# POOL multiplies the gates into nine of sixteen one-hot batches, and the first group of expert blocks takes no fetched rows

## The reference, cut to what matters

```python
q = (xb @ w_query).reshape(tb, PEER_HEADS, 2, PEER_HALF)           # 8 heads, two halves of 128
s = jnp.einsum('thpc,hpnc->thpn', q, sub_keys)                     # 128 keys per half
top_s, top_i = lax.top_k(s, PEER_TOPK)                             # 16 best of each half
cand_s = top_s[:, :, 0, :, None] + top_s[:, :, 1, None, :]         # 16 x 16 sums
best_s, best_pos = lax.top_k(cand_s, PEER_TOPK)                    # 16 best pairs
idx = jnp.take_along_axis(cand_i, best_pos, axis=-1)               # expert = key0 * 128 + key1
g = jax.nn.softmax(best_s, axis=-1)
h = gelu(jnp.einsum('thkd,td->thk', expert_u[idx], xb))
out = jnp.einsum('thk,thkd->td', g * h, expert_v[idx])             # 128 experts per token
```

## Time and profile before

| what | before |
|---|---|
| median of 3 runs | 2973.97 us |
| profiled execution, its own time | 2976.31 us |
| its span, first to last instruction | 2974.5 us |
| PE busy | 2643.6 us (89%) |
| DVE busy | 2434.8 us (82%) |
| ACT busy | 871.1 us (29%) |
| POOL busy | 1254.2 us (42%) |
| mean granted clock of TensorE | 0.939 |

### The profile page before, as it was taken

One profiled execution on the slowest core, in us unless ns is written; L12 is line 12 of the kernel. 1 busy time (PEld: TensorE's weight loads), 2 busy tenths in 40 slices (PEclk: granted clock), 3 DMA queues, 4 the chain that ended last, 5 costly groups with the idle time before them and its releaser, 6 DMA issues.

```text
span 2974.5 us, 47235 instructions
## 1 busy us (share of the span) xinstructions
PE 2643.6 (89%) x17293; PEld 1732.6 (58%) x17459; DVE 2434.8 (82%) x4517; ACT 871.1 (29%) x1463; POOL 1254.2 (42%) x833
## 2 busy tenths in 40 slices
PE   8999888698867674589999999999999999999996
PEld 3566655458867663445555555555555555555553
DVE  3244545574999999589999999999999999999998
ACT  2333333211114444522222222222222222222223
POOL 2110000210000000066666666676667677776772
PEclk9999979799988985689999999999999999999998
DMA  4000010261002223699999999999999999999994
GB/s 153 22 15 15 15 71 15 93 244 48 1 1 114 113 103 160 251 374 351 361 350 353 342 357 344 338 356 347 335 345 337 348 331 350 342 337 338 335 333 177
DMA packets 262960, 685.26 MB, mean 230 GB/s; under 512 B 35624, under 2 KB 118184, under 8 KB 258352
## 3 DMA queue, kind: packets, MB, share of 16 engines
q0 software_dynamic: 110592, 402.70, 36.2%
q1 hardware_dynamic: 152240, 280.98, 26.9%
HBM read 624.89 MB, written 58.72 MB: 230 GB/s over the span
## 4 chain that ended last, share of the span: by engine, by line
PE 20%; issue 13%; DVE 11%; DMA 10%; POOL 2%; SPq 1%; DVEq 0%; ACT 0%; POOLq 0%
PE o_psum L1879 10%; PE h_psum L1861 10%; DMA early<-v_blocks,pick_index 6%; DMA fetched<-v_blocks,pick_index 3%; DVE wide L1731 3%; DVE early L1727 2%; DVE early L1702 2%; DVE v_split L1713 1%; POOL early L1670 1%; DVE wide L1719 1%; DMA fetched<-u_rows,pick_index 1%; DVE act_out L1690 1%; DVE w_split L1694 1%; SPq L2009 1%; POOL fetched L1670 1%
## 5 line engine op out<-in xcount | busy, mean ns | idle before, releaser
L1861 PE MATMUL h_psum<-early 128*128 128x384 bf16 (+1 forms) x6144 | 863.2, 301 | 25.5 <-issue 14.9
L1879 PE MATMUL o_psum<-v_split,w_split 128*128 128x512 bf16 x3713 | 826.9, 380 | 24.6 <-DVE wide L1719 13.4
L1861 PEld LDWEIGHTS h_psum<-early 128*128 128x128 bf16 x6144 | 604.0, 98 | 284.2 <-issue 31.7
L1879 PEld LDWEIGHTS o_psum<-v_split,w_split 128*128 128x128 bf16 x3840 | 375.4, 98 | 456.3 <-DVE wide L1719 18.5
L1670 POOL DMA_INDIRECT early<-v_blocks,pick_index x320 | 488.7, 1527 | 225.4 <-DVE wide L1731 137.4
L1670 POOL DMA_INDIRECT early<-u_rows,pick_index x320 | 448.3, 1401 | 320.1 <-DVE dots L1727 201.5
L1731 DVE SCALAR_TENSOR_TENSOR wide<-early,dots,wide 128x1024 f32<-128x1024 f32 x320 | 402.2, 1282 | 37.3 <-DMA early<-v_blocks,pick_index 33.6
L1727 DVE CUSTOM_DVE_ANT_0 early<-early,wide 128x1024 f32<-128x1024 f32 x320 | 382.1, 1217 | 36.5 <-DMA early<-u_rows,pick_index 31.5
L1617 ACT ACTIVATE w_split<-act_out 128x640 bf16<-128x640 f32 x128 | 94.3, 737 | 633.5 <-DVE act_out L1690 582.2
L1604 ACT ACTIVATE act_out<-h_psum 128x384 f32<-128x384 f32 (+1 forms) x256 | 97.6, 433 | 597.1 <-PE h_psum L1861 546.9
L1101 PE MATMUL r_t_psum<-rt_x_t,early 128*128 128x128 f32 (+1 forms) x1920 | 236.7, 285 | 0.0
(11 more groups left out here) (201 smaller groups left out, 2976.3 us busy)
## 6 DMA issues: line engine op xcount, KB each, us to landing
early<-u_blocks SPq DMA_DIRECT2D x128, 512.0 KB
early<-v_blocks SPq DMA_DIRECT2D x128, 512.0 KB
gates<-wide SPq DMA_DIRECT2D x20, 2048.0 KB, 6.4
gate<-gates SPq DMA_DIRECT2D x32, 1280.0 KB
early<-w_query SPq DMA_DIRECT2D x8, 1024.0 KB, 5.8
att_w_raw<-w_fox SPq DMA_DIRECT2D x4, 1536.0 KB, 6.8
early<-u_rows,pick_index POOLq DMA_INDIRECT x320
early<-v_blocks,pick_index POOLq DMA_INDIRECT x320
```

The lines of the kernel that those rows point to most:

```text
L1861: mm = pe.matmul(h_psum[k][:, half, 0:width * P], u_split[:, k, part, c], xs[:, first:first + width, xpart, c, :], start=(c == 0 and part ...
L1879: mm = pe.matmul(o_psum[(DENSE * p + t) % 2][:, half * 512:half * 512 + 512], w_split[:, p, q, part, t * P:(t + 1) * P], v_split[:, p, q, ...
```

## The change

**Routing.** In the four steps that also hold picks, POOL takes over the multiplication by the gates: for batches 0, 1, 2 and 15 whole (2048 elements), for batches 4 to 8 its low half (1024 elements), and DVE keeps the high half. PE waits for the new semaphore `hot_by_pool` as well. DVE keeps the is_equal of all batches, and everything of the fifth tile.

**Experts.** No row is taken in the first group. From unit 5 on (`FIRST_UNIT`) the 384 U rows are spread evenly to unit 82 (`MIDDLE_UNIT`), and the 384 V rows from there to unit 160. The six first fetches are issued as early as before. DVE's program for the 32 groups is now written out, with no loop.

```diff
+        POOL_BOTH, POOL_LOW = (0, 1, 2, 15), (4, 5, 6, 7, 8)
...
                 def gate_batch(d, m):
                     n = SLOTS * d + m
-                    pe.wait_ge(hot_made, n + 1)
+                    if m in POOL_SLOTS and shared(d):
+                        pe.wait_ge(hot_by_pool, len(POOL_SLOTS) * d + POOL_SLOTS.index(m) + 1)
...
+                def gate_batch(d, m):
+
+                    n, slot, first = SLOTS * d + m, m % HOTS, 0 if m in POOL_BOTH else 1
+                    pool.wait_ge(high_made, n + 1)
+                    pool.tensor_tensor(hot[:, slot, 2 + first:4],
+                                       hot[:, slot, 0].unsqueeze(1).broadcast_to(
+                                           [P, 2 - first, BATCH // 2, N_KEYS, 2]),
+                                       by_pair(gates_t[:, m, first:2].rearrange("p k n -> p (k n)")).rearrange(
+                                           "p (k j) n two -> p k j n two", k=2 - first), ALU.mult
+                                       ).then_inc(hot_by_pool, 1)
...
+                    if m in POOL_BOTH and shared(d):
+                        return
+                    halves = 1 if m in POOL_LOW and shared(d) else 2
                     dve.wait_ge(high_made, n + 1)
...
+    WEIGHED = GROUP * groups // 2 + 2
+    FIRST_UNIT, MIDDLE_UNIT = DENSE, DENSE * (WEIGHED // GROUP) + WEIGHED % GROUP
...
+                def due(unit):
+
+                    if unit <= FIRST_UNIT:
+                        return 0
+                    if unit <= MIDDLE_UNIT:
+                        return TAKES // 2 * (unit - FIRST_UNIT) // (MIDDLE_UNIT - FIRST_UNIT)
+                    return TAKES // 2 + TAKES // 2 * (unit - MIDDLE_UNIT) // (DENSE * groups - MIDDLE_UNIT)
...
-                dve.wait_ge(acc_in, 16 * GATHERED)
-                pair(0, "U")
-                with dve.Fori(1, TURNS) as i:
-                    pair(i, "U")
-                pair(TURNS, "V")
-                with dve.Fori(TURNS + 1, last) as i:
-                    pair(i, "V")
-                pair(last, "V")
+                taken = [0]
+                for g in range(groups):
+                    group_of_blocks(g)
```

More of the change, by code:

```diff
@@ L1263, in step @@
                     for m in range(SLOTS):
[L1264 to L1269, removed]
+                        if not (isinstance(d, int) and d == DENSE):
+                            if m == PRODUCTS_SLOT - 3:
+                                products(t)
+                            if m == PRODUCTS_SLOT - 2:
+                                float_index(t)
+                        if m in POOL_SLOTS and shared(d - 1):
+                            gate_batch(d - 1, m)
                 pool.sem_inc(floated, 1)
@@ L1720, in add, with take @@
                                              ).then_inc(o_added, 1)
[L1722 to L1727, removed]
+                def take(n):
+                    tile, i, k, row = n % GATHERED, n // PICKS, n % PICKS // GATHERED, fetched[n % RING]
+                    dve.wait_ge(fetched_in[n % RING], 16 * (n // RING + 1))
+                    if n < TAKES // 2:
+                        dve.tensor_tensor_reduce(row, row, acc[:, tile], 1.0, 0.0,
@@ L1744, in load_dots, with take_until @@
                     dve.wait_ge(weights_copied, i - TURNS + 1)
[L1746 to L1751, removed]
-                    for q in range(GROUP):
-                        gate_block(GROUP * g + q, g, p, q, n)
-                        split_u_lo(i, GROUP * g + q + 2, GROUP * p + q)
-                        split_v_lo(GROUP * g + q, p, q, GROUP * i + (GROUP * p + q) // 2 + 1)
-                        if p == 0 and q == 0 and kind == "V":
-                            load_dots(i)
+                def take_until(last_take):
+                    for n in range(taken[0], last_take):
+                        if n == 0:
+                            dve.wait_ge(acc_in, 16 * GATHERED)
+                        if n >= TAKES // 2 and n % PICKS == 0:
+                            load_dots(n // PICKS)
+                        take(n)
+                    taken[0] = max(taken[0], last_take)
@@ L1758, in step @@
                         for t in DOWN_TILES[q]:
-                            units += 1
-                            upto = (half * units - half // 2) // DENSE
-                            for r in range(taken, upto):
-                                take(i, kind, half * p + r)
+                            take_until((due(unit) + due(unit + 1)) // 2)
                             if t == DOWN_TILES[q][0]:
-                                split_w_lo(GROUP * g + q, p, q)
-                            if not (first and p == 0):
-                                if t == 0 and first:
+                                split_w_lo(b, p, q)
@@ L1767, in step @@
+                            if g > 0:
+                                if t == 0 and g == 1:
                                     dve.wait_ge(dense_in, 16 * DENSE)
@@ L1769, in step @@
                                     dve.wait_ge(o_added, DENSE * (g - 1))
[L1770 to L1783 removed]
+                                add(g - 1, 1 - p, t, ALPHA if g == 1 else 1.0)
+                            unit += 1
+                            take_until(due(unit))
                 def weigh():
```

63 lines of the change are left out of this document (34 added, 29 removed).

## The result

| what | before | after |
|---|---|---|
| median of 4 runs each, same chip | 2976.97 us | 2947.49 us |
| lowest and highest | 2970.5 to 2981.79 | 2942.5 to 2952.44 |
| profiled execution, own time | 2976.31 us | 2942.5 us |
| its span | 2974.5 us | 2940.7 us |
| mean granted clock | 0.939 | 0.942 |

The ratio is 0.9898 with the interval [0.9874, 0.9922]: 1.0% faster, where I had said 2972 us, in a range of 2952 to 2994. The forecast was wrong.

The account below looks back on a forecast made before the run. DVE was taken to set the routing's pace, transfers the experts' start, and DVE to be no less tight than PE afterwards. Routing -3.7 and experts +2.4 gave -1.3 us on 2976.3, so 2972 us as median, range 2952 to 2994.

Parts of the forecast that it names:

- The rival that POOL's products cost DVE nothing: Routing: DVE and POOL take no turns, so -25 us, 2951 us as median; chance 0.08.
- my own chain of slots 0 to 2: Routing, batches 0 to 2: is_equal 1.2, plus 0.1, plus POOL's product 4.25 gives 5.6 us between is_equals.
- what the sums and the cast take from DVE where they cut in: Routing, batches 3 and 4: POOL's late sums and cast delay DVE by their full length, +1.5 and +0.9 us.
- slot 15: Routing: batch 15's product lies beside the next step's first maxima and searches, -1.2 us in three of four steps.
- -3.7: Whole routing: -3.2 over four steps, -3.6 for batch 15's covered products, +3.1 for the uncovered one, in us.
- the fourth step's last product: End of the fourth routing step: batch 15 has no cover, POOL ends it 3.1 us later than DVE would, +3.1.
- The rival of no earlier landing: Experts' start: V block 2 lands no earlier, PE and DVE gain 16 us instead of 22, 2979 us; chance 0.07.
- DVE's work on the takes moved in: Experts: the 24 takes moved out of the start come back over 31 groups at 1.175 us each, +28.2 us.
- waits for fetched rows: Experts: the 24 moved takes wait 0.1 us each for their rows, at the present mean, +2.4 us.
- other idle time: Experts: DVE gives back 3.2 us of waits for ACT and 2.8 us of gaps without a releaser, -6.0.
- the start's gain is kept: Experts: PE stays the bound in the U half, DVE's row waits shrink; -14 us, 2956 as median; chance 0.20.

Follow-up runs that it names:

- the old places: Changed kernel with takes spread 4.8 a unit from the first unit and the U/V turn at the block of before: 2952.0 us, ratio 0.9903.
- the experts alone: Changed kernel with the old routing, so only the experts' part of the change: 2974.94 us, ratio to the kernel before 0.9975.
- the spread from unit 0: Changed kernel without the first group's rest from takes, the U rows over 82 units instead of 77: 2958.59 us, ratio to before 0.9935.

## Why the prediction was wrong, step by step

**Right: who sets the pace, and that the two engines take turns.** DVE set the pace of the routing before and after. It and POOL exclude each other; DVE goes first where both are released at once (1108.49 and 1108.53 in the rows of the fourth step); the searches leave POOL alone (16 products of 3.60 us beside them). The rival that POOL's products cost DVE nothing would have had the right time, about, for the wrong reason: the fifth tile on POOL lost 12.5 us.

**The step that failed most: what POOL's instructions cost DVE.** Distances from one is_equal to the next in the fourth step, in us:

| slot | before | forecast | measured |
|---|---|---|---|
| 0, 1, 2 | 6.56, 5.50, 7.31 | 5.6, 5.6, 5.6 | 5.52, 4.23, 5.84 |
| 3, 4 | 2.68, 3.81 | 4.2, 4.7 | 3.37, 3.71 |
| 5 to 8 together | 16.85 | 16.2 | 15.28 |

A step gained 4.75 us over its fifteen slots where I had 0.8: 4 steps by 4.0 are 16 of the 23 us that I missed in the routing. Two terms are in it. The first is the price of a product. I took 4.25 us from a bf16 product of another pattern and felt safe since the sums of candidates gave the same 2.07 ns an element. Both were strangers to this instruction; it took 3.60. I had put the lower bound at 4.0 us, with no row that excluded less. With 3.6 in my own chain of slots 0 to 2 (1.2 + 0.1 + 3.6 = 4.9 an is_equal to the next) they give -1.2 - 0.6 - 2.0 = -3.8 us a step instead of -2.5; the trace has -3.8 too, though slot by slot -1.0, -1.3 and -1.5, so the chain holds as a sum. The halves, priced at 2.13, took 1.75; slots 5 to 8 gained 1.6 where I had 0.7.

The second term is what the sums and the cast take from DVE where they cut in. I charged slots 3 and 4 their full length, 0.85, 0.95 and 0.7 us. The three stretched instructions (1.67, 1.75 and 1.65 us) stood still for 0.46, 0.53 and 0.44. Slots 3 and 4 lost 0.6 us together where I had 2.4. My own rows had said so: of the 3.67 us in the earlier trace rows the two sums ran 0.77 and 0.70 us by my reading, and not the 1.85 that they took alone. These shares are worked out from the trace; no run changed the one price without the other.

**The row not read: DVE's idle time at the turn of the loop.** The earlier trace rows gave DVE 76.26 us of a step of 79.35. I called that the bound and did not ask what the other 3.1 were. Two thirds of them are the 1.9 to 2.2 us at each turn, which went with the multiplication: slot 15 was worth 3.3 us a step, not 1.2, three times 2.1, 6.3 us. The loop written out (7.0 us) and batch 15 put back (9.6) show it. So -3.7 becomes -3.7 - 16 - 6.3 = -26.0, and -26.7 with the fourth step's last product at +2.4 instead of +3.1, which is what the trace has. These 6.3 us were luck: the change was not made for them, and why the turn became short is not known.

**Right: the start of the experts.** Block 4's gate product came 22.4 us earlier (22.2 forecast), PE's `up` of block 5 13.4 (14). V block 2 was used 5.5 us earlier (6). The rival of no earlier landing is out.

**Mis-sized: what the moved takes cost.** From block 4 to block 124 I had +24.6 us. The stretch grew by 15.0 on the mean (1574.8 us in five profiles without the rest, 1589.8 in seven with it). The terms, forecast and mean:

| term | forecast | measured |
|---|---|---|
| DVE's work on the takes moved in | +28.2 | +24.8 (1481.5 to 1506.4, 23 takes more) |
| waits for fetched rows | +2.4 | -3.2 (78.4 to 75.2) |
| other idle time | -6.0 | -6.6 (14.8 to 8.2) |

The first term is clear of the spread. The second is not: the waits lie at 73.0 to 90.8 us without the rest and at 63.3 to 81.2 with it, and in the pair of profiles of before and after they rose, from 73.0 to 76.0. So it is not shown that they shrink when DVE comes late. A U group took 52.46 us after (786.9 / 15; 52.8 forecast, 51.78 before), a V group 53.53 (53.8; 52.97 before), with PE idle 1.0 us in each (1.8 forecast). From the mean of the five profiles to that of the seven the U groups grew by 0.9 us and the V groups by 0.15. The rival "the start's gain is kept", with 0.20, came in by some 9 of its 14 us, by the profiles; the medians say from 5.5 (the old places) over 7 (the experts alone) to some 12 (the spread from unit 0).

**A base that was not the mean.** The profile of before, from which I forecast, had the shortest experts of its kind, 1734.4 us; the four other profiles without the rest had 1738.1 to 1750.8. Against it the changed kernel's experts win 1.1 us, against the mean of five (1741.1) the seven with the rest win 8.8 (1732.3). The ratio of the experts alone, 7 us, stands beside the second figure.

The sum of what was measured, -26.7 and -7 to -9, is -34 to -36 us; the ratios of the changed kernel say -30 and -33.

**Open.** Why the branch of DVE's loop takes 2.9 us before, 3.5 with batch 15 put back and 0.3 in the changed kernel. That DVE only comes to the branch early in the changed kernel, while work is still queued, does not suffice: the changed kernel's branch began 2.1 us before the first search (1006.76 to 1008.83), and one of 2.9 us would have left a gap. The loop's body has 313 instructions in the trace before, 307 with batch 15 put back and 305 in the changed kernel, and the loops of ACT (93) and POOL (12 to 30) turn in 0.2 us, so the length and place of the code are a candidate; it was not tested.

## What to carry to other kernels

An engine that sets the pace and is idle for 4% of a step has a cause for those 4%: look for it before any edit is priced, for a change may remove it without meaning to. A price taken from another access pattern has a range on both sides, and the lower end is multiplied by as many instructions as the upper. A forecast made from one profile takes over what that execution had by chance, here some 7 us of the experts. In this kernel, work given to POOL was covered where it stood beside DVE's searches, and was paid for, 12.5 us in the fifth tile, where only is_equals and multiplications stood beside it.

## What was not expected of the hardware

The turn of a loop on DVE took 2.9 to 3.2 us from the branch to the next instruction before, 3.5 to 3.6 with batch 15 put back, and 0.3 in the changed kernel; DVE stood idle for 1.9 to 2.9 us at the long turns and not at all at the short ones. The Trainium skill says that a taken branch out of the fetched window stalls the engine for the fetch and that kernels should be written out where they can (Runtime: NRT & Kernel Launch, Instruction fetch mechanics). The written-out loop agrees by its 7 us. No run here shows whether the short turns of 0.3 us are branches inside that window.

On POOL, a bf16 product whose inputs are both broadcast views took 1.76 ns an element, another bf16 product 2.07.

The experts of one and the same code differ from profile to profile by more than a small change is worth: 1725.2 to 1736.8 us in seven profiles, with the DMA engines 96 to 97% busy.
